# Later low parts of weights, latent key rotation on GpSimd, and attention tiles of layer B in one row

## The chip, the cores and the metric

The kernel runs on one core of a Trainium2 chip. The metric is the time of one execution on the device, in microseconds (us); several runs are taken and their median counts. Besides, the hardware profiler records one execution; all rows below are from that record. TensorE (PE) does the matrix products, VectorE (DVE) and ScalarE (ACT) the work on rows of 128 partitions, GpSimd (POOL) some arithmetic, SyncE (SP) issues the transfers.

## What is computed

512 tokens of width 1024 go through two blocks: layer A (mLSTM and a memory attention), layer B (latent attention and a memory attention), then a second block with differential attention, cross attention and an MLP. The change lies for the most part in layer B. Cut to that layer:

```python
def shared_kv(x, positions, kv_norm, w_kv_a, kv_lat_norm, w_kv_b, k_gain):
    h = rmsnorm(x, kv_norm)
    c_kv, k_pe = split_cols(h @ w_kv_a, [KV_LORA, QK_ROPE])            # 256, 64
    kv = (rmsnorm(c_kv, kv_lat_norm) @ w_kv_b).reshape(bsz, s, B_HEADS, QK_NOPE + V_HEAD)
    k_nope, v = kv[..., :QK_NOPE], kv[..., QK_NOPE:]
    k = jnp.concatenate([k_nope, broadcast(k_pe)], axis=-1)
    k = rmsnorm(k, k_gain)
    return concatenate([k[..., :QK_NOPE], rope(k[..., QK_NOPE:], positions)]), v

def mla_layer(x, positions, k_sh, v_sh, ...):
    h = rmsnorm(x, norm_g)
    q_lat, z, mq, mz = split_cols(h @ w_in, [Q_LORA, B_WIDTH, MEM_WIDTH, MEM_WIDTH])
    q = (rmsnorm(q_lat, q_lat_g) @ w_q_up).reshape(bsz, s, B_HEADS, QK_HEAD)   # 8 heads
    q = rmsnorm(q, q_gain);  q = concatenate([q[..., :QK_NOPE], rope(q[..., QK_NOPE:], positions)])
    attn = chunk_causal_attention(q, k_sh, v_sh)     # tiles of 128 queries, keys up to the tile's end
    y_b = attn * silu(z)
    y_mem = memory_attention(mq, mz, mk, mv, mq_gain)                            # 4 heads, 256 keys
    return x + concatenate([y_b, y_mem]) @ w_out
```

## The kernel before, in words

Every product with a weight is computed at nearly float32 accuracy from two fp32r parts. A weight chunk (two blocks of 128 rows, up to 512 columns) is fetched into one of two raw buffers, ScalarE writes its high part (step `split`, line 1549, in two halves), and VectorE the low part, raw minus high (line 1938, `sb_w_split<-sb_raw,sb_w_split`, in two halves, each waiting for ScalarE's half). TensorE then does three matmuls per block of rows and output tile: high by high, high by low, low by high (lines 1246 to 1248 or 1251 to 1253). There are three buffers for split chunks, so the split of chunk n+2 stands at the start of chunk n; the fetch into a raw buffer waits for the low part that was made from it.

One list of steps, made by `order_of_work` with the class `Plan`, sets the order on all five engines: each engine walks through the list and does its share of each step, in order. `Plan.product` puts the rows of a product, and after some of them calls `Plan.step`, which may put a step from one of two side lanes. A side step goes in when what it needs stands in the list already and a distance (`lag`, in a planner's nanoseconds of TensorE work) from the last one is reached. If a product needs the result of side steps that aren't in the list yet, `need` forces them in, one after the other, with no rows between.

The side work of layer B:

- `rounds` lays out an attention tile by tile. A tile's scores (`msc` of the memory attention, `asc` of the latent attention) are computed on TensorE into one of PSUM banks 4 to 7, VectorE takes the row maximum (line 2153) and scales it (1941), ScalarE takes the exponential (step `exp`, line 1695), VectorE divides by the sum (`norm`, lines 2159 and 1941), TensorE turns the result over (`mtp`, `atp`, line 1209) and ScalarE copies it out. A round holds the turning of tile n-2, `norm` of tile n-1 and the scores of tile n; `exp` of tile n stands a distance later. When a head's four tiles are turned, its values product (`mval` at line 1345, `aval` at 1425) follows, then VectorE's product with the gate and the two parts of y (`ysplit`). `mem_b` and `mla` call `rounds` once for each pair of heads, so each pair ends with three rounds without new scores.
- Each pair of latent heads has a preparation in seven steps, `prep0` to `prep6`, in the other lane: sums of squares on ScalarE (line 1517, four squares each in prep0 to prep3), transposes of q and k on TensorE, normalisation on VectorE, and rotation of q's last 64 columns on GpSimd (prep4 and prep5, line 2441). prep6 turns the rotated q over; ScalarE copies it out in two halves. The scores of the pair's first tile wait for all of these copies.
- `kpe` rotates the 64 shared key columns for all four token tiles, on VectorE.

Products in the order of the list: qlB, ckvB, mk1, mqB, mv1, mzB0, mzB1, kvB0, quB0, zB0, kvB1, quB1, zB1, kvB2, quB2, zB2, kvB3, quB3, zB3, outB0, outB1. outB takes y's 12 blocks of 128 in the order 0 to 3, 8 to 11, 4 to 7; blocks 0 to 7 are the heads' values.

## Time and profile before

| what | us |
|---|---|
| median of 3 runs (lowest, highest) | 1583.37 (1582.98, 1588.41) |
| the profiled execution | 1586.22 |
| its span from first to last instruction | 1584.4 |
| TensorE busy in the span | 1535.1 (97%) |
| VectorE, ScalarE, GpSimd busy | 887.2, 707.6, 223.0 |

An engine's idle time costs only where the engine that sets the end waits for it. TensorE is the one that is nearly always busy, so a row of TensorE with a bracket, the idle time ahead of it and what ended it, is the thing to look for. Transposes and single matmuls are pipelined, so the gap between starts is some 0.17 us more than the idle time in the bracket.

### The profile page before, as it was taken

How to read it: one execution, taken by the hardware profiler on the slowest of the kernel's cores; microseconds unless marked ns; L12 is line 12 of the kernel's file. 1: busy time of each engine (PE TensorE's matmuls, PEld its weight loads, DVE VectorE, ACT ScalarE, POOL GpSimd, SP SyncE). 2: the span in 40 equal slices, each digit the busy share in tenths (PEclk: the TensorE clock that was granted, in tenths of full speed). 3: DMA queues.
4: the chain of work that ended last, by engine and by line, in shares of the span. 5: the costliest groups of instructions: out<-in, count | busy, mean ns of one | idle time of the engine just before them, and what ended most of it. 6: DMA issues, size and time to landing. Idle time of an engine off the chain costs nothing.

```text
span 1584.4 us, 19220 instructions
## 1 busy us (share of the span) xinstructions
PE 1535.1 (97%) x7128; PEld 1245.0 (79%) x7128; DVE 887.2 (56%) x1747; ACT 707.6 (45%) x1611; POOL 223.0 (14%) x192
## 2 busy tenths in 40 slices
PE   7999999999999999999899999999999999999997
PEld 5887778887898777777588877788778888888886
DVE  6467485657465566666457567664446433444343
ACT  6554343334355767665334444443344423333241
POOL 3202020202120003222022005120002000000001
PEclk9999999999999999999999999999999999999998
DMA  6522122323424221112133221233232333333331
GB/s 193 160 67 80 53 81 67 94 67 120 119 74 142 81 61 55 52 57 67 41 120 100 87 67 54 67 116 111 93 93 68 107 100 100 93 94 106 94 94 66
DMA packets 89069, 141.04 MB, mean 89 GB/s; under 512 B 6417, under 2 KB 36497, under 8 KB 88977
## 3 DMA queue, kind: packets, MB, share of 16 engines
q1 hardware_dynamic: 88256, 139.02, 28.8%
q8 instruction: 56, 0.92, 0.2%
q10 hardware_dynamic: 720, 0.81, 0.2%
q14 instruction: 37, 0.30, 0.1%
HBM read 137.71 MB, written 2.10 MB: 88 GB/s over the span
## 4 chain that ended last, share of the span: by engine, by line
PE 78%; DVE 9%; ACT 5%; issue 3%; POOL 3%; DMA 2%; SPq 0%; POOLq 0%; ACTq 0%; DVEq 0%
PE banks L1246 16%; PE banks L1248 16%; PE banks L1247 16%; PE banks L1251 6%; PE banks L1253 6%; PE banks L1252 6%; DVE sb_w_split L1938 2%; PE banks L1209 2%; DVE sb_arena L1947 2%; ACT sb_junk L1517 2%; PE banks L1372 1%; ACT sb_w_split L1549 1%; PE banks L1425 1%; PE banks L1488 1%; DVE sb_arena L1941 1%
## 5 line engine op out<-in xcount | busy, mean ns | idle before, releaser
L1938 DVE TENSOR_TENSOR sb_w_split<-sb_raw,sb_w_split 128x512 fp32r<-128x512 f32 (+4 forms) x530 | 344.4, 692 | 365.5 <-ACT sb_w_split L1549 364.8
L1549 ACT ACTIVATE sb_w_split<-sb_raw 128x512 fp32r<-128x512 f32 (+4 forms) x530 | 288.1, 592 | 424.3 <-PE banks L1248 307.7
L1246 PE MATMUL banks<-sb_actA,sb_w_split 128*128 128x512 f32 x672 | 276.4, 411 | 2.4 <-DVE sb_arena L1938 2.1
L1248 PE MATMUL banks<-sb_actA,sb_w_split 128*128 128x512 f32 x672 | 263.1, 392 | 0.0
L1247 PE MATMUL banks<-sb_actA,sb_w_split 128*128 128x512 f32 x672 | 262.1, 390 | 0.0
L1246 PE MATMUL banks<-sb_actB,sb_w_split 128*128 128x512 f32 (+1 forms) x640 | 248.5, 388 | 1.5 <-DVE sb_actB L1938 1.5
L1248 PE MATMUL banks<-sb_actB,sb_w_split 128*128 128x512 f32 (+1 forms) x640 | 242.9, 380 | 0.0
L1247 PE MATMUL banks<-sb_actB,sb_w_split 128*128 128x512 f32 (+1 forms) x640 | 242.6, 379 | 0.0
L1251 PE MATMUL banks<-sb_w_split,sb_actA 128*128 128x512 f32 (+1 forms) x384 | 153.7, 400 | 13.3 <-DVE sb_w_split L1938 9.9
L2458 POOL TENSOR_TENSOR sb_arena<-sb_arena 128x512 f32<-128x512 f32 x43 | 63.4, 1474 | 686.5 <-ACT sb_arena L1590 684.1
L1246 PEld LDWEIGHTS banks<-sb_actA,sb_w_split 128*128 128x128 f32 x672 | 126.5, 188 | 32.3 <-issue 7.2
L1252 PE MATMUL banks<-sb_w_split,sb_actA 128*128 128x512 f32 (+1 forms) x384 | 149.3, 389 | 0.0
L1253 PE MATMUL banks<-sb_w_split,sb_actA 128*128 128x512 f32 (+1 forms) x384 | 149.3, 389 | 0.0
L1248 PEld LDWEIGHTS banks<-sb_actA,sb_w_split 128*128 128x128 f32 x672 | 126.2, 188 | 27.3
L1247 PEld LDWEIGHTS banks<-sb_actA,sb_w_split 128*128 128x128 f32 x672 | 126.7, 189 | 24.5 <-issue 1.0
L1246 PEld LDWEIGHTS banks<-sb_actB,sb_w_split 128*128 128x128 f32 x640 | 120.6, 188 | 26.1 <-issue 2.5
L1247 PEld LDWEIGHTS banks<-sb_actB,sb_w_split 128*128 128x128 f32 x640 | 120.7, 189 | 22.8 <-issue 1.4
L1248 PEld LDWEIGHTS banks<-sb_actB,sb_w_split 128*128 128x128 f32 x640 | 120.5, 188 | 22.8
L2449 POOL TENSOR_TENSOR sb_small<-sb_small,sb_cons 128x4 f32<-128x4 f32 (+3 forms) x30 | 42.1, 1404 | 548.9 <-DVE sb_small L1944 548.9
L1251 PEld LDWEIGHTS banks<-sb_w_split,sb_actA 128*128 128x128 f32 x384 | 72.9, 190 | 27.6 <-issue 13.7
L1253 PEld LDWEIGHTS banks<-sb_w_split,sb_actA 128*128 128x128 f32 x384 | 73.0, 190 | 14.4
L1251 PE MATMUL banks<-sb_w_split,sb_actB 128*128 128x512 f32 (+2 forms) x208 | 81.9, 394 | 2.4 <-DVE sb_w_split L1938 1.6
(217 smaller groups left out, 2084.7 us busy)
## 6 DMA issues: line engine op xcount, KB each, us to landing
sb_raw<-in_a_w_in SPq DMA_DIRECT2D x66, 256.0 KB, 3.0
sb_raw<-in_w_up SPq DMA_DIRECT2D x32, 512.0 KB, 3.7
sb_raw<-in_w_down SPq DMA_DIRECT2D x32, 512.0 KB, 3.8
sb_raw<-in_w_in SPq DMA_DIRECT2D x24, 512.0 KB, 3.6
sb_raw<-in_mem_w_kv SPq DMA_DIRECT2D x16, 512.0 KB, 3.8
sb_raw<-in_w_ckv SPq DMA_DIRECT2D x16, 512.0 KB, 3.7
sb_raw<-in_a_w_in SPq DMA_DIRECT2D x15, 512.0 KB, 3.8
sb_raw<-in_a_w_out SPq DMA_DIRECT2D x12, 512.0 KB, 3.8
```

The source lines that it names most:

```text
L1209: t = pe.op.transpose(v.ps[0:rows, place.bank, n * P:(n + 1) * P], block, v.ident)
L1246: pe.op.matmul(out, hi[:, cs], x.hi(k), start=i == 0, stop=False)
L1247: pe.op.matmul(out, hi[:, cs], x.lo(k), start=False, stop=False)
L1248: t = pe.op.matmul(out, lo[:, cs], x.hi(k), start=False, stop=last_i)
L1251: pe.op.matmul(out, x.hi(k)[:, cs], hi, start=i == 0, stop=False)
L1252: pe.op.matmul(out, x.hi(k)[:, cs], lo, start=False, stop=False)
L1253: t = pe.op.matmul(out, x.lo(k)[:, cs], hi, start=False, stop=last_i)
L1517: t = act.op.activation(v.junk[:, 0:src.shape[-1]], src, ACT.Square, accum_out=out)
L1549: act.op.activation(hi[:, cs], raw[:, cs], ACT.Copy).then_inc(act.mark(m("w_hi"), 2 * n + part + 1), 1)
L1938: dve.op.tensor_tensor(out, a, b, op).then_inc(dve.mark(*mark) if mark else dve.tick(), 1)
L2449: pool.op.tensor_tensor(v.stat(root, n), v.stat(mean, n), v.con("minus_half", 0, n), ALU.pow).then_inc(m.at("rstd", step)[0], 1)
L2458: pool.op.tensor_tensor(total, total, v.square_of(norm, n)[1], ALU.add).then_inc(pool.mark(signal, value), 1)
```

## The change

Four edits of the list, and one step on another engine.

1. A new step `low` does VectorE's low part; `split` keeps ScalarE's high part. `low` of a chunk goes into the list at the next call of `Plan.step`, ahead of the next side step, or at the latest ahead of the next `split`. For products with 256 tokens it stays at once behind `split`.
2. `kpe` runs on GpSimd: one product with the gain over all four tiles in place of four, then the same six operations of the rotation.
3. `mla` and `mem_b` call `rounds` once over all heads. What a tile needs (its pair's prep6) is asked for tile by tile.
4. Lags of the preparation: prep0 2600 in place of 4000, prep6 5000 in place of 6500, the others 1600 in place of 2600.

```diff
+    def low(self):
+
+        if self.held_low is not None:
+            self.put(("low", self.held_low))
+            self.held_low = None
+
     def step(self):
+        self.low()
         if self.soon:
...
+                self.low()
                 self.put(("split", self.n_split))
+                self.held_low = self.n_split
+                if pr.tokens < SEQ:
+                    self.low()
...
-            needed = list(after) if n == 0 else []
+            needed = list(after(*units[n])) if n < len(units) else []
...
-    def mla(h0):
-        rounds(0, [(h, j) for h in (h0, h0 + 1) for j in range(TT)], "asc", "atp",
-               lambda u: [("aval", *u), ("ysplit", "yB", *u)], [("prep6", h0 // 2)],
+    def mla():
+        rounds(0, [(h, j) for h in range(B_HEADS) for j in range(TT)], "asc", "atp",
+               lambda u: [("aval", *u), ("ysplit", "yB", *u)], lambda h, j: [("prep6", h // 2)],
...
-    def mem_b(h0):
-        rounds(0, [("B", h, i) for h in (h0, h0 + 1) for i in range(TT)], "msc", "mtp", lambda u: [("mval", *u)],
-               [("hnscale", "mqB"), ("hnt", "mk1", 3)], [("silu", f"mzB{h0 // 2}", 1)], lag=1300, wait=1000)
+    def mem_b():
+        rounds(0, [("B", h, i) for h in range(MEM_HEADS) for i in range(TT)], "msc", "mtp", lambda u: [("mval", *u)],
+               lambda layer, h, i: [("hnscale", "mqB"), ("hnt", "mk1", 3)],
+               lambda u: [("silu", f"mzB{u[1] // 2}", 1)], lag=1300, wait=1000)
...
-            p.side(1, after, (f"prep{n}", q), lag={0: 4000, 6: 6500}.get(n, 2600))
+            p.side(1, after, (f"prep{n}", q), lag={0: 2600, 6: 5000}.get(n, 1600))
...
     (vector_program)
-        if kind == "split":
+        if kind == "low":
...
-        elif kind == "kpe":
-            g = v.prob[:, 0, 0:TT * QK_ROPE].rearrange("p (i n) -> p i n", i=TT)
-            gain = v.rows[:, ROW["k_gain_pe"]:ROW["k_gain_pe"] + QK_ROPE]
-            for i in range(TT):
-                dve.wait_ge(*m.evicted("ckvB", i))
-                tensor(g[:, i, :], v.ckv[:, i, KV_LORA:320], gain, ALU.mult)
-            dve.settle()
-            dve.wait_ge(*m.at("cos", ("rotab2",)))
-            rope(g, v.kpe, v.prob[:, 1, 0:TT * HALF].rearrange("p (i n) -> p i n", i=TT), v.cosB, v.sinB,
-                 *m.at("kpe", step))
     (gpsimd_program)
+        elif kind == "kpe":
+            g = v.prob[:, 0, 0:TT * QK_ROPE].rearrange("p (i n) -> p i n", i=TT)
+            tmp = v.prob[:, 1, 0:TT * HALF].rearrange("p (i n) -> p i n", i=TT)
+            gain = v.rows[:, ROW["k_gain_pe"]:ROW["k_gain_pe"] + QK_ROPE]
+            pool.wait_ge(m("dma_params"), 48)
+            for i in range(TT):
+                pool.wait_ge(*m.evicted("ckvB", i))
+            pool.settle()
+            tensor(g, v.ckv[:, :, KV_LORA:320], gain.unsqueeze(1).broadcast_to([P, TT, QK_ROPE]), ALU.mult)
+            pool.settle()
+            pool.wait_ge(*m.at("cos", ("rotab2",)))
+            s1, s2, o1, o2 = g[:, :, 0:HALF], g[:, :, HALF:], v.kpe[:, :, 0:HALF], v.kpe[:, :, HALF:]
+            tensor(o1, s1, v.cosB, ALU.mult)
+            tensor(tmp, s2, v.sinB, ALU.mult)
...
+            tensor(o2, o2, tmp, ALU.add, *m.at("kpe", step))
```

What that makes of the order, at three places. The first is TensorE at the end of outB0, the last tiles of head 7 (`atp` is line 1209, `asc` 1408, 1410 and 1225, `aval` 1425, rows of outB0 1246 to 1248). Before:

```order
L1209 MATMUL banks<-sb_cons,sb_arena 128x128
L1408 MATMUL banks<-sb_arena 128x384
L1410 MATMUL banks<-sb_arena 128x384
L1225 MATMUL banks<-sb_masks 128x128
L1209 MATMUL banks<-sb_cons,sb_arena 128x128 x2
L1408 MATMUL banks<-sb_arena 128x512
L1410 MATMUL banks<-sb_arena 128x512
L1225 MATMUL banks<-sb_masks 128x128
L1209 MATMUL banks<-sb_cons,sb_arena 128x128 x7
L1425 MATMUL banks<-sb_arena 128x512
...
L1246 MATMUL banks<-sb_actB,sb_w_split 128x512
```

Now, from the second tile's `atp` on (the same code is at lines 1222, 1421, 1423, 1238, 1438 and 1259 to 1261):

```order
L1222 MATMUL banks<-sb_cons,sb_arena 128x128 x2
L1421 MATMUL banks<-sb_arena 128x512
L1423 MATMUL banks<-sb_arena 128x512
L1238 MATMUL banks<-sb_masks 128x128
L1259 MATMUL banks<-sb_actB,sb_w_split 128x512
...
L1222 MATMUL banks<-sb_cons,sb_arena 128x128 x3
L1259 MATMUL banks<-sb_actB,sb_w_split 128x512
...
L1222 MATMUL banks<-sb_cons,sb_arena 128x128 x4
L1259 MATMUL banks<-sb_actB,sb_w_split 128x512
...
L1438 MATMUL banks<-sb_arena 128x512
```

Between the steps of the last tiles there were no rows of the product; now there are four rows (of three matmuls each) after the last scores, two after `atp` of three blocks and two after that of four. `aval` of head 7 stood directly behind `atp`, with the chunk's first row after it; now the last row of the chunk before and then that first row follow it.

The second place is VectorE while TensorE is at mzB1 and kvB0, in the memory attention's first tiles (`norm` is 2159 and the 1941 with 128x256, the maximum 2153, low parts `sb_w_split`). Before:

```order
L2153 TENSOR_REDUCE sb_small<-banks 128x1
L1941 TENSOR_SCALAR sb_small<-sb_small 128x1
L1938 TENSOR_TENSOR sb_w_split<-sb_raw,sb_w_split 128x384 x2
L2159 RECIPROCAL sb_small<-sb_small 128x1
L1941 TENSOR_SCALAR sb_actB_plain<-sb_actB_plain,sb_small 128x256
L2153 TENSOR_REDUCE sb_small<-banks 128x1
L1941 TENSOR_SCALAR sb_small<-sb_small 128x1
L1938 TENSOR_TENSOR sb_arena<-sb_arena,sb_rows 128x64 x4
...
L1938 TENSOR_TENSOR sb_arena<-banks,sb_arena 128x512 x2
L1947 SCALAR_TENSOR_TENSOR sb_arena<-sb_cons,sb_arena 128x512
L2159 RECIPROCAL sb_small<-sb_small 128x1
```

Now, at the same tiles:

```order
L2166 TENSOR_REDUCE sb_small<-banks 128x1
L1954 TENSOR_SCALAR sb_small<-sb_small 128x1
L2172 RECIPROCAL sb_small<-sb_small 128x1
L1954 TENSOR_SCALAR sb_actB_plain<-sb_actB_plain,sb_small 128x256
L2166 TENSOR_REDUCE sb_small<-banks 128x1
L1954 TENSOR_SCALAR sb_small<-sb_small 128x1
L1951 TENSOR_TENSOR sb_w_split<-sb_raw,sb_w_split 128x384 x2
L1951 TENSOR_TENSOR sb_arena<-banks,sb_arena 128x512 x2
L1960 SCALAR_TENSOR_TENSOR sb_arena<-sb_cons,sb_arena 128x512
L2172 RECIPROCAL sb_small<-sb_small 128x1
```

The low part moved behind the next `norm` and maximum, into the place where the ten operations of `kpe` stood.

The third place is TensorE at the start of outB0, where the last pair's prep6 (four transposes) stands. Before:

```order
L1225 MATMUL banks<-sb_masks 128x128
L1246 MATMUL banks<-sb_actB,sb_w_split 128x512
L1247 MATMUL banks<-sb_actB,sb_w_split 128x512
L1248 MATMUL banks<-sb_actB,sb_w_split 128x512
L1209 MATMUL banks<-sb_cons,sb_arena 128x128 x4
L1246 MATMUL banks<-sb_actB,sb_w_split 128x512
...
L1209 MATMUL banks<-sb_cons,sb_arena 128x128 x2
L1408 MATMUL banks<-sb_arena 128x512
```

Now:

```order
L1259 MATMUL banks<-sb_actB,sb_w_split 128x512
L1260 MATMUL banks<-sb_actB,sb_w_split 128x512
L1261 MATMUL banks<-sb_actB,sb_w_split 128x512
L1222 MATMUL banks<-sb_cons,sb_arena 128x128 x7
L1421 MATMUL banks<-sb_arena 128x128
L1423 MATMUL banks<-sb_arena 128x128
L1238 MATMUL banks<-sb_masks 128x128
```

prep6 stood in outB0 behind the scores of tile 2 of head 5, and the scores of head 6, which wait for its copies, came 12 rows later. Now prep6 follows outB0's first four rows, and behind its four transposes come three of an `atp` and at once head 6's first scores.

## Rows read from the trace of the kernel before

**Rows 1.** The page, busy time per engine: busy us (share of the span) xinstructions.

```profile
PE 1535.1 (97%) x7128; PEld 1245.0 (79%) x7128; DVE 887.2 (56%) x1747; ACT 707.6 (45%) x1611; POOL 223.0 (14%) x192
```

**Rows 2.** Waits of TensorE, 545 to 790 us: line, releaser, total, times, longest.

```profile
PE banks L1209 <- DVE sb_arena L1941: 6.3, 6, 2.2
PE banks L1209 <- DVE sb_actB_plain L1941: 6.0, 6, 1.7
```

**Rows 3.** Timeline, end of outB0: start, duration, instruction, xcount, [idle before it].

```profile
768.06 2.32 PE L1425 MATMUL banks<-sb_arena 128*128 128x512 f32 x8
...
773.28 0.44 PE L1209 MATMUL banks<-sb_cons,sb_arena 128*128 128x128 f32 x2 [1.44 <-DVE sb_arena L1941]
...
778.21 0.66 PE L1209 MATMUL banks<-sb_cons,sb_arena 128*128 128x128 f32 x4 [2.15 <-DVE sb_arena L1941]
779.64 4.09 PE L1425 MATMUL banks<-sb_arena 128*128 128x512 f32 x8 [0.78 <-ACT sb_arena L1816]
...
783.76 0.69 DVE L1947 SCALAR_TENSOR_TENSOR sb_arena<-banks,sb_arena 128x512 f32<-128x512 f32 x1 [5.62 <-PE banks L1425]
...
785.90 0.50 PE L1246 MATMUL banks<-sb_actB,sb_w_split 128*128 128x512 f32 x1 [1.47 <-DVE sb_actB L1938]
```

**Rows 4.** The chain that ended last, in order of time: one matmul of outB0.

```profile
764.97 0.23 PE banks L1247
```

**Rows 5.** Stretch at that place: us, busy per engine, granted clock (PEclk).

```profile
780.00:785.00 5.00, 4.43 (x11) 2.22 (x9) 0.69 (x1) 0.51 (x1) 0.00 (x0) 0.68 0.01 3
```

**Rows 6.** Timeline, mzB1 and kvB0: VectorE, then TensorE.

```profile
557.35 1.03 DVE L1938 TENSOR_TENSOR sb_w_split<-sb_raw,sb_w_split 128x384 fp32r<-128x384 f32 x2 [1.20 <-ACT sb_w_split L1549]
...
559.33 0.62 DVE L1938 TENSOR_TENSOR sb_arena<-sb_arena,sb_rows 128x64 f32<-128x64 f32 x4
559.99 1.68 DVE L1938 TENSOR_TENSOR sb_arena<-sb_arena 128x128 f32<-128x128 f32 x6
...
551.32 0.44 PE L1209 MATMUL banks<-sb_cons,sb_actB_plain 128*128 128x128 f32 x2 [0.76 <-DVE sb_actB_plain L1941]
...
555.62 0.44 PE L1209 MATMUL banks<-sb_cons,sb_actB_plain 128*128 128x128 f32 x2 [1.35 <-DVE sb_actB_plain L1941]
...
564.17 0.44 PE L1209 MATMUL banks<-sb_cons,sb_actB_plain 128*128 128x128 f32 x2 [1.67 <-DVE sb_actB_plain L1941]
```

**Rows 7.** GpSimd, whole span, groups by line and form: products of two tensors.

```profile
L2480 POOL TENSOR_TENSOR sb_arena<-sb_arena 128x496 f32<-128x496 f32 x4 | 5.0, 1249 | 0.3
...
L2477 POOL TENSOR_TENSOR sb_arena<-sb_arena 128x16 f32<-128x16 f32 x4 | 0.9, 222 | 0.3
```

**Rows 8.** Timeline, zB2: VectorE and GpSimd at the same time.

```profile
675.93 2.33 DVE L1938 TENSOR_TENSOR sb_w_split<-sb_raw,sb_w_split 128x384 fp32r<-128x384 f32 x2
...
676.91 5.63 POOL L2441 TENSOR_TENSOR sb_arena<-sb_arena 128x256 f32<-128x256 f32 x6
```

**Rows 9.** Timeline of TensorE, zB0 and zB2: the longest idle of each.

```profile
599.81 0.44 PE L1209 MATMUL banks<-sb_cons,sb_actB_plain 128*128 128x128 f32 x2 [1.72 <-DVE sb_actB_plain L1941]
...
672.38 0.44 PE L1209 MATMUL banks<-sb_cons,sb_arena 128*128 128x128 f32 x2 [1.07 <-DVE sb_arena L1941]
```

**Rows 10.** Groups by line and form, ScalarE, zB2 (656 to 679 us).

```profile
L1517 ACT ACTIVATE sb_junk<-sb_arena 128x192 f32<-128x192 f32 x8 | 2.9, 363 | 0.5
L1807 ACT ACTIVATE sb_arena<-banks,sb_cols 128x512 f32<-128x512 f32 x4 | 2.7, 670 | 0.0
```

**Rows 11.** Timeline of GpSimd, last pair: from the sums of q on.

```profile
716.68 2.01 POOL L2449 TENSOR_TENSOR sb_small<-sb_small,sb_cons 128x8 f32<-128x8 f32 x1 [5.62 <-DVE sb_small L1944]
...
720.02 6.24 POOL L2441 TENSOR_TENSOR sb_arena<-sb_arena 128x256 f32<-128x256 f32 x6
```

**Rows 12.** Stretch of zB2: busy per engine (PE PEld DVE ACT POOL), clock, DMA.

```profile
656.00:679.00 23.00, 21.84 (x107) 16.19 (x106) 13.89 (x32) 16.76 (x58) 6.92 (x6) 1.00 0.19 61
```

**Rows 13.** Timeline, end of ozA0 in layer A: VectorE, then TensorE.

```profile
134.08 4.29 DVE L1938 TENSOR_TENSOR sb_w_split<-sb_raw,sb_w_split 128x512 fp32r<-128x512 f32 x4
...
141.41 0.69 PE L1251 MATMUL banks<-sb_w_split,sb_actA 128*128 128x512 f32 x1 [2.98 <-DVE sb_arena L1947]
```

More of the change, by code:

```diff
@@ L378, in advance @@
                 self.take(lane)
+    def low(self):
+        if self.held_low is not None:
+            self.put(("low", self.held_low))
+            self.held_low = None
     def step(self):
+        self.low()
         if self.soon:
@@ L478, in finish @@
         total = len(self.chunks)
-        self.order = [s for s in self.order if s[0] not in ("split", "fetch") or s[1] < total]
+        self.order = [s for s in self.order if s[0] not in ("split", "low", "fetch") or s[1] < total]
         self.chunk_of = {c: n for n, c in enumerate(self.chunks)}
@@ L545, in order_of_work @@
     p.put(("split", 0))
+    p.put(("low", 0))
     p.put(("fetch", 2))
@@ L549, in order_of_work @@
     p.put(("split", 1))
+    p.put(("low", 1))
     p.n_split, p.n_fetch = 2, 3
@@ L584, in order_of_work @@
     rounds(0, units, "msc", "mtp", lambda u: [("mval", *u)],
-           [("hnscale", "mqA"), ("silu", "mzA", 3), ("hnt", "mk0", 3)], lag=6000)
+           lambda layer, h, i: [("hnscale", "mqA"), ("silu", "mzA", 3), ("hnt", "mk0", 3)], lag=6000)
     def mlstm_head(h):
@@ L662, in latents @@
             after = [("asc", 2 * q - 3, TT - 1)] if q >= 2 and n == 0 else [("ysplit", "yB", 3)] if (q, n) == (3, 4) else ()
-            p.side(1, after, (f"prep{n}", q), lag={0: 4000, 6: 6500}.get(n, 2600))
+            p.side(1, after, (f"prep{n}", q), lag={0: 2600, 6: 5000}.get(n, 1600))
     def gated(name):
         p.product(name, (), lambda j: [(("silu", name, j),)])
-    mem_b(0)
-    mem_b(2)
+    mem_b()
     p.need(("nrow", "b"))
@@ L675, in order_of_work @@
     gated("zB0")
-    for n in range(4):
-        mla(2 * n)
+    mla()
     latents(1)
@@ L758, in order_of_work @@
         for n in (2 * g, 2 * g + 1):
-            rounds(n % 2, [(n, i) for i in range(TT)], "csc", "ctp", lambda u: [("cval", *u)], (),
+            rounds(n % 2, [(n, i) for i in range(TT)], "csc", "ctp", lambda u: [("cval", *u)], lambda h, i: (),
                    [("ev", f"cvD{g}", MT - 1)])
@@ L2482, in gpsimd_program @@
             pool.op.tensor_tensor(u[:, 0:16], edge, u[:, 0:16], ALU.subtract).then_inc(pool.mark(*m.at("pooled", step)), 1)
+        elif kind == "kpe":
[12 more added lines that the diff above has]
+            tensor(tmp, s2, v.sinB, ALU.mult)
+            pool.settle()
+            tensor(o1, o1, tmp, ALU.subtract)
+            tensor(o2, s2, v.cosB, ALU.mult)
+            pool.settle()
+            tensor(tmp, s1, v.sinB, ALU.mult)
+            pool.settle()
+            tensor(o2, o2, tmp, ALU.add, *m.at("kpe", step))
         elif kind in ("prep4", "prep5"):
```

## The prediction

> **What bounds the kernel now.** I began with the page: TensorE is busy in 1535.1 of 1584.4 us, no other engine in more than 56% of the span [rows 1]. The change removes no work of TensorE, so all that it can give or take is TensorE's idle time, some 49 us in all, and the question is which waits lie where the order changes. The waits of TensorE in layer B come next [rows 2]: two kinds make up 12.3 us, the turning of a latent tile (`atp`) that waits for VectorE's `norm`, and the same for the memory attention (`mtp`), six times each. The timeline then shows where these stand. The end of outB0 is the worst place [rows 3]: idle times of 1.44, 2.15, 0.78 and 1.47 us follow one another, because head 7's last steps are forced in with no rows of the product between them. In a single matmul's price, 0.23 us [rows 4], a row of the product is 0.69 us, so there is room to fill. The idle time costs more than itself: the granted clock over the next 5 us is 0.68 on average [rows 5], so the engine spent part of that stretch at the lower of its two levels (1.2 and 2.4 GHz) after having stood idle, and head 7's values product took 4.09 us where head 6's took 2.32 [rows 3]. The other places are the start of the memory attention [rows 6], the z products [rows 9], and the end of ozA0 in layer A [rows 13].
>
> **The tail of outB0.** Before: idle 1.44 + 2.15 + 0.78 + 1.47 = 5.8, a short wait of 0.2 more, and 4.09 - 2.32 = 1.8 in the slow values product; 7.8 together. Now four rows (2.8 us) stand behind the last scores. From the start of the scores in question to the `atp` that needs them TensorE now takes 773.28 to 778.21, that is 4.9 us, of which 2.15 were waited; 2.8 us of rows cover that wait. The tile before gets rows as well, and the two rows (1.4 us) between the last `atp` and the values product cover the 0.78 for ScalarE's copy. What is left is the wait for y's last block: from the end of the values product (779.64 + 4.09 = 783.73) to 785.90 is 2.17 us, of which two rows now fill 1.38. That leaves 0.8 idle, and 0.17 more between starts, so 0.95. With the long idle times gone I take the clock to stay up. Gain 7.8 - 0.95 = 6.9; from 6.0, if the clock still falls for half of that product, to 7.6.
>
> **The start of the memory attention, mzB1 and kvB0.** Four `mtp` wait here; three of them are in [rows 6], with 0.76, 1.35 and 1.67, and a shorter one stands between; with the 0.17 between starts, 4.8 us. The low part (1.03) and `kpe` (0.62 + 1.68) stand ahead of the `norm` in question. For the last two of the four, moving the low part behind the next maximum and taking 2.3 us of `kpe` off VectorE is more than the wait, so both go: -2.3. The first two stay: they wait for the exponential's own chain, not for a low part of their own. Against it stands `kpe` on GpSimd, which the trace doesn't show. The nearest rows are products of 496 columns at 1.25 and of 16 at 0.22 us [rows 7], which by a straight line puts one of 256 at 0.75 and the six of 128 at 0.45 each: 3.5 us (1.5 if all cost 0.22, 8.8 if all cost 1.25). It starts after the gate's sums, where VectorE has low parts with two operands in SBUF to do. Such a low part takes 2.33 us in two halves while GpSimd rotates [rows 8], and 1.03 while it is idle [rows 6]: 0.65 for each half. One to two halves fall into `kpe`'s time: +0.65 to +1.3 at the first tile, I take 1.1. Gain 1.2; from a loss of 0.5, if the last two are late for another reason (the exponential), to 3, if nothing collides.
>
> The Trainium skill ("SBUF — State Buffer", Who interferes with whom) says that a VectorE instruction with two SBUF inputs and a GpSimd instruction that reads SBUF exclude one another, the later one being stopped for the whole of the other. The 2.33 against 1.03 agrees in kind. It speaks against this part of the change: by the full stop, two halves and two products of the gate would lose up to 1.25 each in `kpe`'s time, the start's gain would be gone, and the sum below would be 5.3 instead of 6.5; the forecast's range holds that.
>
> **The z products.** In zB0, one `mtp` waits 1.72 us [rows 9] and another 0.2; with the pairs in one row, the scores of head 3's first tile now follow without a break, and need the bank that ScalarE's exponential of the tile four back empties, behind a denser preparation: I put that wait at 1.9 against 2.3 now. Gain 0.4; from -1.9 (both waits stand) to 1.9. In zB1, waits below 0.4 us go in part: gain 0.4 (0 to 1).
>
> In zB2, before: an `atp` waits 1.07 [rows 9], with short ones 1.5 in all. Now prep1's sums of squares stand ahead of a tile's exponential, and the scores of the next pair's first tile stand directly behind prep6's four transposes. ScalarE has to copy these out first: two copies at 0.67 [rows 10], a third operation of that size ahead of them, and 0.2 for the hand-over, so 2.2. The tile behind prep1's four squares (0.36 each, 1.45 together [rows 10]) is late by half of that, 0.75; with a short one of 0.35 the stage has 3.3. Loss 1.8; from a gain of 1 to a loss of 3.5.
>
> In zB3 and the start of outB0, GpSimd is the chain: from the sums of q at 716.68 to the rotated q at 726.26 (720.02 + 6.24) it takes 9.6 us [rows 11], and 1.9 us go by on TensorE, ScalarE and VectorE ahead of that: 11.5 us from prep3. The order wants prep6 some 9.3 us of TensorE's work behind prep3 (its rows and side steps at their prices). The distances of prep4 to prep6 add up to 8.2 us now and to 11.7 before. So TensorE waits about 2.0 at prep6, and then about 1.1 for the copies, as in zB2 with something between; it has 1.6 now, of which one `atp` with 1.06. Loss 1.5; from a gain of 1.2, if GpSimd is as quick as in the first pair, to a loss of 3.5.
>
> Denser preparation also puts more low parts beside GpSimd's rotation: two halves more at 0.65 [rows 8, 6], of which 1.0 reaches TensorE (0 to 1.5).
>
> **Layer A and the rest.** At the end of ozA0, VectorE does four halves of low parts in 4.29 us, and the eviction that TensorE waits for comes after; 2.98 idle [rows 13]. The low part of one chunk moves behind that eviction: 2.1 us less ahead of it, of which the exponential's own chain gives back a little. Gain 2.0 with a short wait of 0.4 nearby (0 to 3.4). Elsewhere the low part has no step of VectorE between it and its old place. Its new place delays the fetch into the raw buffer by less than one side step, and SP's queue holds nothing else that TensorE waits for there; TensorE wants the low part two chunks later. I cost this at nothing; what hides it is that distance. If it were gone, a row would wait for a low part, some 1.0 us each.
>
> **The sum.** -6.9 (tail) - 1.2 (start) - 0.4 (zB0) - 0.4 (zB1) + 1.8 (zB2) + 1.5 (zB3) + 1.0 (beside GpSimd) - 2.0 (layer A) = -6.6. Against the profiled execution, 1586.22, that is 1579.6. It stood 2.85 above the median of the runs, so I forecast a median of 1577.0, which is 0.4% faster.
>
> **Rivals.**
> First, the shorter distances cost nothing: prep6 arrives in time, and the three losses of zB2, zB3 and GpSimd (4.3) don't appear, while the waits that both stages have now (1.5 and 1.6) go. Then -6.6 - 4.3 - 3.1 = -14.0, or 1569.4. For it speaks that TensorE idles only 1.2 us of the 23 in zB2 now [rows 12] with ScalarE at 16.8; against it, that GpSimd's 9.6 us [rows 11] are longer than the new distance.
>
> Second, only the tail counts: the low part's and `kpe`'s moves turn into waits for the next thing on the same chain. Then the tail's -6.9 and the losses of +4.3 stand alone: -2.6, or 1581. For it speaks that the first `mtp` waits are there with no low part ahead of them; against it, the order on VectorE, where `norm` now stands ahead.
>
> Third, slower: ScalarE becomes the bound in the z stages. It is busy in 16.8 of 23 us of zB2 [rows 12]. There are 16 groups of four squares (four pairs, prep0 to prep3), 1.45 us each [rows 10]. If each now falls directly ahead of a tile's exponential, so that the two rounds between scores and turning no longer hide it, TensorE waits 16 x 1.45 = 23.2 us, less the two waits near 1.07 that it has now, less the tail's 6.9: +14, or 1597.6. It decides from the point where a round's work on TensorE is shorter than a group, an exponential and `norm` together; a round with its rows is some 3 us, so most groups fit.
>
> Fourth, the change doesn't do what it says, because the new order leaves the tail's forced steps; the order on TensorE shows rows there, so I give it no chance of its own.
>
> **How the numbers follow.** The forecast's case (1574 to 1580) gets 0.50, the first rival (1567 to 1574) 0.22, the second (1580 to 1583) 0.22, the third 0.06. About 0.5% is what a measurement of this kernel can tell from no change: 1575.45 and 1591.3 are the bounds. Faster is the first rival and a third of the forecast's case, 0.38; slower the third, 0.06; the same the rest, 0.56. The range leaves out the lower half of the first rival, the upper end of the second and the third: 1571 to 1582.
>
> **What would show it.** In the profile after, no idle time over 1 us should stand in the last 15 us of outB0, head 7's values product should take about 2.3 us, and a wait near 0.8 should stand for y's last block. At mzB1 and kvB0 two `mtp` waits should be gone, and low parts longer than 1.03 should lie beside GpSimd's `kpe` of some 3.5 us. At the last pair's prep6 a wait for GpSimd of about 2 us should stand, and one for ScalarE's copies at the scores behind it; without these the first rival is right. Waits for ScalarE at most of the tiles in the z stages would show the third. The prediction is wrong if a new wait of several us stands where the order didn't change, or if the clock falls at a place where it didn't before.

## The result, and the profile after

The changed kernel takes 1592.41 us (median of 9 runs, 1588.94 to 1594.43), the kernel before 1586.53 (9 runs, 1582.98 to 1589.63): a ratio of 1.0042, 95% interval 1.0032 to 1.0052. By that ratio it is slower by 6.7 us; 1577.0 was forecast, and the range ended at 1582. The profiled execution's span grew from 1584.4 to 1591.3 us, by 6.9.

The page, against [rows 1]:

```profile
PE 1540.6 (97%) x7128; PEld 1246.4 (78%) x7128; DVE 887.1 (56%) x1737; ACT 708.2 (45%) x1611; POOL 227.1 (14%) x199
```

Waits of TensorE from 545 to 800 us of the changed kernel (line, releaser, total, times, longest), against [rows 2]:

```profile
PE banks L1222 <- DVE sb_actB_plain L1954: 3.7, 3, 1.9
PE banks L1222 <- DVE sb_arena L1954: 2.5, 3, 1.4
PE banks L1344 <- ACT sb_actB_plain L1708: 1.8, 1, 1.8
PE banks L1421 <- ACT sb_actB_plain L1818: 1.5, 1, 1.5
PE banks L1222 <- POOL sb_arena L2444: 1.5, 1, 1.5
PE banks L1421 <- ACT sb_arena L1818: 1.4, 1, 1.4
PE banks L1259 <- DVE sb_arena L1951: 1.2, 1, 1.2
PE banks L1222 <- DVE sb_arena L1951: 0.8, 1, 0.8
```

The two kinds of [rows 2], 6.3 and 6.0, are down to 2.5 and 3.7. New kinds stand beside them: scores (L1344, L1421) that wait for ScalarE, prep6 (L1222) for GpSimd, rows for an eviction.

The tail of outB0, timeline of TensorE, against [rows 3]:

```profile
784.75 0.49 PE L1222 MATMUL banks<-sb_cons,sb_arena 128*128 128x128 f32 x3
...
788.30 2.32 PE L1438 MATMUL banks<-sb_arena 128*128 128x512 f32 x8
...
792.79 0.51 PE L1259 MATMUL banks<-sb_actB,sb_w_split 128*128 128x512 f32 x1 [0.78 <-DVE sb_actB L1951]
```

This part came out as forecast. No `atp` waits, the last values product takes 2.32 in place of 4.09, and 0.78 us are left ahead of y's last block.

To see where more than these 7 us went, I took each matmul's distance to the next one, less the median distance for its kind, and summed this over the list's stages. The sums explain the spans: 57.6 and 64.4 us, a difference of 6.8. Kinds can be told apart in more than one way, which moves a difference of the table by up to 0.4. In us:

| stage | before | changed | difference | forecast |
|---|---|---|---|---|
| layer A | 9.4 | 12.9 | +3.5 | -2.0 |
| qlB to mv1 | 2.8 | 3.4 | +0.6 | 0 |
| mzB0 to quB0 | 5.3 | 4.0 | -1.3 | -1.2 |
| zB0 to quB1 | 2.7 | 5.2 | +2.5 | -0.4 |
| zB1 to quB2 | 2.0 | 2.7 | +0.7 | -0.4 |
| zB2 to quB3 | 2.5 | 5.7 | +3.2 | +1.8, and +1.0 beside GpSimd |
| zB3 and outB0's first 28 rows | 3.4 | 9.3 | +5.9 | +1.5 |
| outB0's last 20 rows | 9.2 | 1.3 | -7.9 | -6.9 |
| from outB1 on | 20.4 | 20.0 | -0.4 | 0 |

From mzB0 on, the stages of layer B repeat within some 0.2 us between executions with the same order there (but for the clock, last section). The first two lines and the last don't. Up to qlB's first matmul, TensorE takes 439.7 us in the kernel before, 438.0 to 441.6 in the nine below that order layer A as it does, 442.0 in e1 and 442.9 in the changed kernel. From outB1's first matmul to the last one it takes 784.0 to 789.1 over all kernels, whose order there differs at most in low parts. So a single profile says much on layer B and little on the rest.

### The profile page after: what moved, and what is told of

It is laid out like the page before. It is cut to its first block, busy times and chain, and to the rows that moved or that the text cites. A ratio compares the mean times of both kernels' runs of the same rounds, so it can differ in the third digit from the quotient of the medians.

```text
span 1591.3 us, 19222 instructions
## 1 busy us (share of the span) xinstructions
PE 1540.6 (97%) x7128; PEld 1246.4 (78%) x7128; DVE 887.1 (56%) x1737; ACT 708.2 (45%) x1611; POOL 227.1 (14%) x199
## 4 chain that ended last, share of the span: by engine, by line
PE 74%; DVE 11%; ACT 6%; issue 4%; POOL 3%; DMA 2%; SPq 0%; POOLq 0%; ACTq 0%; DVEq 0%
PE banks L1259 16%; PE banks L1261 16%; PE banks L1260 16%; PE banks L1264 5%; PE banks L1266 5%; PE banks L1265 5%; DVE sb_w_split L1951 4%; DVE sb_arena L1960 3%; ACT sb_junk L1530 3%; PE banks L1222 2%; PE banks L1385 1%; ACT sb_w_split L1562 1%; DVE sb_arena L1954 1%; PE banks L1501 1%; PE banks L1421 1%
## 5 line engine op out<-in xcount | busy, mean ns | idle before, releaser
L1951 DVE TENSOR_TENSOR sb_w_split<-sb_raw,sb_w_split 128x512 fp32r<-128x512 f32 (+4 forms) x530 | 353.5, 708 | 220.5 <-ACT sb_w_split L1562 220.0
L1264 PEld LDWEIGHTS banks<-sb_w_split,sb_actA 128*128 128x128 f32 x384 | 73.5, 191 | 28.2 <-issue 12.2
L1951 DVE TENSOR_TENSOR sb_x_res<-sb_x_res,banks 128x512 f32<-128x512 f32 x64 | 43.9, 686 | 91.7 <-PE banks L1261 91.7
```

What stands on the lines that cost most here:

```text
L1264: pe.op.matmul(out, x.hi(k)[:, cs], hi, start=i == 0, stop=False)
L1951: dve.op.tensor_tensor(out, a, b, op).then_inc(dve.mark(*mark) if mark else dve.tick(), 1)
```

## The experiments

All ratios are to the kernel before, from runs on the same chip; the medians of before were 1586.04 (e1 to e4), 1586.24 (e5 to e7), 1586.11 (e8 to e10) and 1584.03 (e11, e12). A ratio compares all runs and need not be that of the medians; two ratios that differ by less than some 0.0017 (2.7 us) are not told apart by these runs. My theory was that each new wait hangs on one edit at its place; the rivals stand in the expectations.

### The edits one by one: e1 to e4

**e1**, the low parts alone (`low` and its calls, VectorE's branch):

```diff
     def step(self):
+        self.low()
         if self.soon:
...
+                self.low()
                 self.put(("split", self.n_split))
+                self.held_low = self.n_split
...
-        if kind == "split":
+        if kind == "low":
```

> The kernel before with only the low parts later. Theory 1 (a later low part falls into chains that TensorE waits for): the waits of the changed kernel in layer A come back here, 2.5 us at head 1's first scores and 0.8 us in vA2, and layer A is 3 to 4 us longer than before; the whole is 2 to 4 us slower, 1588 to 1591 beside 1586.5. Rival (those waits come from one execution to the next, not from the order): layer A as before within 1 us, and the whole within 1 us of before.

Measured: 1590.23, ratio 1.0031 (1.0019 to 1.0043). Theory 1 holds. The waits in layer A are back, 2.54 and 0.71 us, and so is one behind ozA0 that I hadn't listed, 2.09 (0.80 in the changed kernel); layer A's sum is 11.9 against 9.4, zB0's 4.3 against 2.7.

**e2**, one row each, with old distances:

```diff
-            needed = list(after) if n == 0 else []
+            needed = list(after(*units[n])) if n < len(units) else []
...
-    for n in range(4):
-        mla(2 * n)
+    mla()
```

> The kernel before with only the attentions of layer B in one row each. Theory 1 (the row pays at the end of outB0, and the losses of the z stages come from the low parts and the shorter distances): the tail's waits go, -7 us, and new waits at the first scores of a pair take 0 to 3 us back, so 3 to 7 us faster, 1579.5 to 1583.5. Rival (the row itself costs in the z stages, since the three rounds without new scores were the slack in which a pair's preparation was done): the tail's 7 us are given back at the pairs' first scores, and the whole is within 1.5 us of before.

Measured: 1590.73, ratio 1.0040 (1.0025 to 1.0055), slower than either expected. The z stages go from 7.2 to 13.2, zB3 with outB0's first 28 rows from 3.4 to 6.9, and the tail keeps 4.0, since with old distances the last tiles still come late; timeline of TensorE there:

```profile
785.53 2.39 PE L1424 MATMUL banks<-sb_arena 128*128 128x512 f32 x8 [1.71 <-ACT sb_arena L1815]
...
790.10 0.50 PE L1245 MATMUL banks<-sb_actB,sb_w_split 128*128 128x512 f32 x1 [1.47 <-DVE sb_actB L1937]
```

So the row itself costs in the z stages, as the rival says, and theory 1's clean tail belongs to row and distances together.

**e3**, the distances alone:

```diff
-            p.side(1, after, (f"prep{n}", q), lag={0: 4000, 6: 6500}.get(n, 2600))
+            p.side(1, after, (f"prep{n}", q), lag={0: 2600, 6: 5000}.get(n, 1600))
```

> The kernel before with only the preparation at shorter distances. Theory 1 (the denser preparation puts ScalarE's squares and copies ahead of tiles): waits at tiles behind the sums of squares of 0.8 us and more appear in zB0, zB1 and zB2, and the whole is 2 to 5 us slower, the tail's 7 us unchanged. Rival (the waits of the z stages come from the row, which leaves no round without new scores): within 1 us of before.

Measured: 1604.90, ratio 1.0121 (1.0107 to 1.0134): 19 us, far more than expected. The z stages go from 7.2 to 23.0. Timelines of VectorE and TensorE in zB2 of e3:

```profile
681.81 0.17 DVE L1944 TENSOR_SCALAR sb_small<-sb_small 128x8 f32<-128x8 f32 x1 [2.86 <-ACT sb_junk L1517]
682.90 1.29 DVE L1938 TENSOR_TENSOR sb_w_split<-sb_raw,sb_w_split 128x512 fp32r<-128x512 f32 x2 [0.33 <-ACT sb_w_split L1549]
684.31 1.16 DVE L1941 TENSOR_SCALAR sb_arena<-sb_arena,sb_small 128x256 f32<-128x256 f32 x1
...
685.52 0.44 PE L1209 MATMUL banks<-sb_cons,sb_arena 128*128 128x128 f32 x2 [1.67 <-DVE sb_arena L1941]
687.10 2.07 PE L1408 MATMUL banks<-sb_arena 128*128 128x512 f32 x2 [1.13 <-ACT sb_arena L1695]
```

VectorE waits 2.86 us for the sums of squares (`sb_junk` is ScalarE's), and behind that wait stand, in its order, a low part and only then the tile's `norm` (684.31); `atp` waits 1.67 us for it, and the next scores for an exponential. This is my third rival's mechanism, ScalarE's squares in front of tiles, reached by way of VectorE. In one row the tiles stand elsewhere between the preparation's steps and it costs less (e5). Shorter distances are not needed for it: in zB2 of e2, with the old ones, VectorE waits 2.86 us for the squares as well, and an `atp` 2.15 behind it:

```profile
683.24 0.18 DVE L1943 TENSOR_SCALAR sb_small<-sb_small 128x8 f32<-128x8 f32 x1 [2.86 <-ACT sb_junk L1516]
...
688.08 0.44 PE L1208 MATMUL banks<-sb_cons,sb_arena 128*128 128x128 f32 x2 [2.15 <-DVE sb_arena L1940]
```

**e4**, the key rotation alone, with the bodies that the diff of the change shows:

```diff
     (vector_program)
-        elif kind == "kpe":
...
     (gpsimd_program)
+        elif kind == "kpe":
```

> The kernel before with only the key rotation on GpSimd. Theory 1 (it takes 2.3 us off VectorE and slows VectorE's work beside it): the fourth wait of the memory attention's start, 1.67 us, goes, the first, 0.76 us, becomes about 1.9; the whole within 1 us of before. Rival (beside GpSimd nothing is slower that TensorE waits for): the first wait stays at 0.8, and the whole is 1.5 to 2.5 us faster.

Measured: 1585.17, ratio 1.0000 (0.9989 to 1.0010). Theory 1 holds to the number; the first `mtp` waits 1.79 in place of the 0.76 of [rows 6], the fourth doesn't wait:

```profile
553.25 0.44 PE L1209 MATMUL banks<-sb_cons,sb_actB_plain 128*128 128x128 f32 x2 [1.79 <-DVE sb_actB_plain L1941]
...
557.56 0.44 PE L1209 MATMUL banks<-sb_cons,sb_actB_plain 128*128 128x128 f32 x2 [1.35 <-DVE sb_actB_plain L1941]
```

### What of it the low parts cost: e5 and e6

**e5** is the changed kernel with each low part beside its high part; **e6** has them at once in layer A only. The edits of the changed kernel, first e5's, then e6's:

```diff
     def step(self):
-        self.low()
         if self.soon:
...
-        if kind == "low":
+        if kind == "split":
```

```diff
-                if pr.tokens < SEQ:
+                if pr.tokens < SEQ or ("enter", "outA1") not in self.done:
                     self.low()
```

> The changed kernel with each low part back beside its high part, the other three edits kept. Theory 1 (the later low parts cost about 3 us in layer A and 1 to 2 in zB0): layer A as in the kernel before, and the whole 3 to 6 us under the changed kernel's 1592.4, so 1586 to 1589, the tail of outB0 still without waits over 1 us. Rival (the low parts' place matters for layer A alone and helps in layer B, where norm stands ahead of them): the start of the memory attention and the z stages get worse by 2 us or more, and the whole is 1590 to 1593.

> The changed kernel with the low parts at once in layer A, later from layer B on. Theory 1 (layer A's new waits come from low parts that moved behind the first eviction of a head, beside GpSimd's products): the wait of 2.5 us at head 1's first scores is back at 1.3 and the one of 0.8 us in vA2 is gone; layer A is 3 us shorter than in the changed kernel, layer B as there, and the whole 1589 to 1590.5. Rival (layer A's waits don't hang on that): layer A and the whole as in the changed kernel, 1591.5 to 1593.5.

Measured: e5 1588.61, ratio 1.0018 (1.0005 to 1.0032); e6 1587.90, ratio 1.0006 (0.9993 to 1.0018). Theory 1 holds for layer A: of the 6.7 us 5.7 go in e6, where the low parts are at once there (3 to 8 by the two intervals). Layer B is not decided. The rival of e5 names the right places, since the start of the memory attention has 4.4 without the later low parts (e5) and 4.0 with them (e6), zB0 5.8 and 5.1, zB2 6.6 and 5.7; but zB3 with outB0's first 28 rows has 6.3 without and 7.9 with them, the clock's fall there included, and the ratios of e5 and e6 are not told apart.

The place in layer A, head 1's first scores; VectorE, GpSimd and TensorE of the changed kernel:

```profile
216.04 2.18 DVE L1951 TENSOR_TENSOR sb_w_split<-sb_raw,sb_w_split 128x512 fp32r<-128x512 f32 x2
...
232.72 3.08 DVE L1951 TENSOR_TENSOR sb_w_split<-sb_raw,sb_w_split 128x512 fp32r<-128x512 f32 x2
...
233.83 1.42 POOL L2573 TENSOR_TENSOR sb_arena<-sb_arena 128x512 f32<-128x512 f32 x1
...
235.40 2.04 PE L1373 MATMUL banks<-sb_arena 128*128 128x512 f32 x2 [2.52 <-POOL sb_arena L2573]
```

and of e6, in which TensorE reaches this place 1.6 us later:

```profile
216.19 1.29 DVE L1951 TENSOR_TENSOR sb_w_split<-sb_raw,sb_w_split 128x512 fp32r<-128x512 f32 x2
...
231.38 1.29 DVE L1951 TENSOR_TENSOR sb_w_split<-sb_raw,sb_w_split 128x512 fp32r<-128x512 f32 x2 [1.30 <-ACT sb_w_split L1562]
...
234.49 1.15 POOL L2573 TENSOR_TENSOR sb_arena<-sb_arena 128x512 f32<-128x512 f32 x1
...
235.79 1.10 PE L1373 MATMUL banks<-sb_arena 128*128 128x512 f32 x2 [1.34 <-POOL sb_arena L2573]
```

In e6 no low part takes over 1.29 here. In the changed kernel one stands at 216.04 beside GpSimd's products of the convolution and takes 2.18, so all that VectorE does behind it is 0.9 us later, down to the step that lets GpSimd begin its last two products; the next, moved behind an eviction, meets the last of these: it takes 3.08, and the product 1.42 in place of 1.15. Together that is the 1.2 us by which the scores wait longer, 2.52 against 1.34. The place repeats well: 2.52 and 2.54 in the two kernels with later low parts here, 1.34 to 1.36 in the twelve others. After the wait the scores run at half the pace (2.04 for two against 1.10; the granted clock is 0.50 from 235.4 to 238.8 us), which e1, with a wait of 2.54, does not show: that part is the clock (last section). In vA2 a low part of 2.18 stands straight ahead of the eviction that TensorE waits for (0.77 us there, 0.71 in e1, nothing in the others).

### The tail without the rest: e7

```diff
-            by_bank = kk > 1 and (last or c == 0 and first)
+            by_bank = kk > 1 and (last and name != "outB0" or c == 0 and first)
...
+            ("atp", 7, 0): 36, ("exp", "asc", 7, 2): 37, ("atp", 7, 1): 38, ("exp", "asc", 7, 3): 39, ("atp", 7, 2): 40,
+            ("atp", 7, 3): 41, ("aval", 7): 42}
...
     p.product("outB0", first=False)
+    spread()
```

`spread` takes the side steps from head 6's first scores on, in their order, and puts each group behind the row of outB0 whose number the table gives.

> The kernel before in which only outB0's last rows are spread between the steps of heads 6 and 7, three or two rows to a tile in place of four and none, and block 6 ahead of block 7; nothing else is moved. Theory 1 (the tail's waits are paid for with rows at hand): of the 7.8 us there some 3 stay, and the whole is 3.5 to 5.5 us faster, 1581 to 1583. Rival (VectorE and ScalarE set the pace of the tiles, and with fewer rows each tile waits): the waits move to the tiles of head 6, and the whole is within 1.5 us of before.

Measured: 1583.34, ratio 0.9977 (0.9966 to 0.9988): faster by 2.9 us in the medians and 3.6 by the ratio, at the lower end of the 3.5 to 5.5 expected. Theory 1 holds: the profile's tail is 4.9 in place of 9.2, and the tiles of head 6 don't wait. Timeline of TensorE there:

```profile
777.18 0.66 PE L1237 MATMUL banks<-sb_cons,sb_arena 128*128 128x128 f32 x4 [1.97 <-DVE sb_arena L1969]
...
783.18 0.50 PE L1274 MATMUL banks<-sb_actB,sb_w_split 128*128 128x512 f32 x1 [1.47 <-DVE sb_actB L1966]
```

The old order of the z stages with rows in the tail beats the whole change.

### The first scores of a pair: e8 and e9

**e8** is e6 with e7's `by_bank` line and a distance between prep6 and a new pair's first scores; **e9** puts the last prep6 later as well:

```diff
-            p.side(lane, needed, *group, lag=lag)
+            pair = scores == "asc" and n and n < len(units) and n % (2 * TT) == 0
+            if pair:
+                p.side(lane, needed, lag=0)
+                needed = []
+            p.side(lane, needed, *group, lag=2000 if pair else lag)
...
-            p.side(1, after, (f"prep{n}", q), lag={0: 2600, 6: 5000}.get(n, 1600))
+            p.side(1, after, (f"prep{n}", q), lag={0: 2600, 6: 5000 + (1500 if q == 3 else 0)}.get(n, 1600))
```

> The kernel of e6 (low parts at once in layer A) in which the first scores of a new pair of heads come at least 2 us of TensorE's work after prep6, and the last block of outB0 follows block 6 whole, so that the tail keeps its rows. Theory 1 (in one row the first scores stand directly behind prep6 and wait for ScalarE's copies): the waits of 1.5 us at head 4's and 1.4 us at head 6's first scores go, GpSimd's wait of 1.5 us at prep6 stays, and the whole is 2 to 3.5 us under e6's 1587.9, 1584.4 to 1586. Rival (ScalarE has too much to do at that place, whatever follows): waits of the same sum appear at the tiles around, and the whole is 1587 to 1589.

> As e8, with the last pair's prep6 1.5 us later. Theory 1 (TensorE stands at prep6 until GpSimd's rotation is done): GpSimd's wait of 1.5 us goes as well; since the last tiles come later, up to 1 us of it comes back in the tail; 1583.5 to 1586. Rival (the rotation itself is late because VectorE's low parts and GpSimd slow each other, and moves on): GpSimd's wait stays over 1 us, and the whole is as e8 or slower.

Measured: e8 1584.66, ratio 0.9991 (0.9982 to 1.0001); e9 1585.57, ratio 0.9999 (0.9989 to 1.0010). For e8 theory 1 holds at most in the sum, by the ratios 2.4 us under e6, which is within the noise, and not in the places. In zB2, head 4's wait is gone, but a tile of head 3 now waits for its exponential. In outB0, head 6's is down from 1.40 to 0.99 only, and prep6's wait for GpSimd, which I expected to stay, is gone; TensorE in zB2 and outB0, then GpSimd:

```profile
677.13 0.70 PE L1425 MATMUL banks<-sb_arena 128*128 128x256 f32 x2 [1.78 <-ACT sb_arena L1712]
...
739.23 0.46 PE L1425 MATMUL banks<-sb_arena 128*128 128x128 f32 x2 [0.99 <-ACT sb_arena L1822]
...
723.70 2.01 POOL L2456 TENSOR_TENSOR sb_small<-sb_small,sb_cons 128x8 f32<-128x8 f32 x1 [5.39 <-DVE sb_small L1961]
```

Moving the tiles of heads 3 and 4 moved the last pair's preparation in the list too: GpSimd begins its part at 723.70, in e6 at 728.92. e9 leaves no wait at head 6 (outB0's head 3.6), and the tail takes it back (5.5): what the preparation gets, the last tiles lose.

### A version that beats both: e10 to e12

**e10** is e7 with `kpe` on GpSimd and low parts later in four products; **e11** is the kernel before with only heads 4 to 7 in one row (the arguments of `mla` are the first head and their count), e8's distance, and the tail spread from head 5's last tiles on; **e12** is e11 with e10's edits:

```diff
-    for n in range(4):
-        mla(2 * n)
+    mla(0, 2)
+    mla(2, 2)
+    mla(4, 4)
...
+                self.held_low = self.n_split
+                if name not in ("qkA0", "mzB1", "kvB0", "gC0"):
+                    self.low()
```

> The kernel of e7 (old order and distances, spread tail) with the key rotation on GpSimd and later low parts in four products alone: qkA0, mzB1, kvB0 and gC0. Theory 1 (each edit pays where no chain that TensorE waits for follows the low part): the last two waits of the memory attention's start go (-1.3 together with the first's growth), the one of 1.9 us at gC0's end shrinks to 0.8, the one of 0.6 us ahead of ozA0 goes; 2 to 3 us under e7's 1583.3, so 1580.3 to 1581.5. Rival (these are below what differs from one execution to the next): 1582.5 to 1584.

> The kernel before (old distances, low parts at once, key rotation on VectorE) with heads 4 to 7 alone in one row, head 6's first scores 2 us of work behind prep6, and outB0's rows spread between the tiles of heads 6 and 7. Theory 1 (in the row the losses come where scores stand directly behind prep6 and where the preparation is dense, the gain from the rows in the tail): the z stages wait as before, no wait over 0.5 us at head 6's first scores, and of the tail's waits 1 to 1.5 us stay; 2 to 4 us under e7, 1579.5 to 1581.5. Rival (the tiles at three rows each wait for VectorE and ScalarE): waits of 1 us and more at the tiles of heads 6 and 7, and the whole as e7, 1583, or slower.

> e11 with the key rotation on GpSimd and later low parts in qkA0, mzB1, kvB0 and gC0, as in e10. Theory 1 (these places pay): 2 to 2.5 us under e11, by 1.3 in the memory attention's start, 0.7 ahead of ozA0 and 0.9 in gC0. Rival (as e10 against e7 showed 0.3 us in the medians, the gains are taken back elsewhere): within 1 us of e11.

Measured: e10 1582.99, ratio 0.9972 (0.9963 to 0.9981); e11 1578.63, ratio 0.9964 (0.9952 to 0.9977); e12 1575.97, ratio 0.9950 (0.9937 to 0.9964), 8 us faster than before and, by the ratios, 0.9% faster than the changed kernel. e11's z stages wait as in the kernel before (2.7, 2.0, 2.5), outB0's first 28 rows 3.5, its tail 1.8. In e12 one wait over 0.3 us is left in outB0; timeline of TensorE:

```profile
777.60 0.50 PE L1294 MATMUL banks<-sb_actB,sb_w_split 128*128 128x512 f32 x1 [0.79 <-DVE sb_actB L1986]
```

On the small edits the runs say little: from e11 to e12 it is 2.7 us by the medians (2.2 by the ratios, as expected), from e7 to e10 0.3 (0.8), and in both cases the intervals overlap. The profiles show that one of the three places gives nothing: the wait ahead of ozA0 (0.40) goes, but the next one, at vA0's first row, grows from 2.97 to 3.64 in e10 and from 2.95 to 3.63 in e12. The other two places are shorter in both.

## Why the prediction failed, step by step

**The tail** was right: 6.9 forecast, 7.9 by the sums, with the 0.95 that was to stay (0.78 idle). One reason given was incomplete. The rows came there from one row and shorter distances together; with one row alone the tail keeps 4.0 (e2). And the 1.8 us for the slow values product hang on the execution that was profiled: e3 has the same four waits in its tail (1.45, 2.16, 0.78, 1.47), a granted clock of 1.00 behind them, and a values product of 2.39.

**The memory attention's start** was right: -1.2 forecast, -1.3 measured, with the last two waits gone and the first longer by 1.1. GpSimd's rotation took 0.88 + 3.71 us where 3.5 was estimated. VectorE beside it is slower by the 1.1 that was taken, but in part by luck: about half of it is a step that the prediction didn't list, two small `TENSOR_SCALAR` that take 0.79 us beside GpSimd's first product and 0.25 in the kernel before. GpSimd, VectorE and TensorE:

```profile
549.48 0.88 POOL L2444 TENSOR_TENSOR sb_arena<-sb_arena,sb_rows 128x256 f32<-128x256 f32 x1
550.43 3.71 POOL L2444 TENSOR_TENSOR sb_arena<-sb_arena 128x128 f32<-128x128 f32 x6
...
549.68 0.79 DVE L1954 TENSOR_SCALAR sb_small<-sb_small 128x16 f32<-128x16 f32 x2
...
556.21 0.44 PE L1222 MATMUL banks<-sb_cons,sb_actB_plain 128*128 128x128 f32 x2 [1.88 <-DVE sb_actB_plain L1954]
```

The rule of the Trainium skill that was weighed there ("SBUF — State Buffer", Who interferes with whom) would have left no gain; the trace shows the collision and, since it met only the first tile, a gain all the same. (By the prediction's own sum of 6.6 the figure without that gain is 5.4, not 5.3.)

**Layer A** was the step with the largest miss: +3.5 against -2.0. Two sentences failed. The first is that at the end of ozA0 the moved chunk leaves "2.1 us less ahead of it", of the eviction, worth a gain of 2.0. The 4.29 us of [rows 13] are not two equal parts: the chunk that stayed takes 3.08 beside GpSimd's products, so only 1.2 went, and 2.43 us are left of the wait of 2.98. And the chunk that moved stands behind the first eviction but ahead of the second, for which TensorE waits next. VectorE and TensorE of the changed kernel:

```profile
140.04 3.08 DVE L1951 TENSOR_TENSOR sb_w_split<-sb_raw,sb_w_split 128x512 fp32r<-128x512 f32 x2
...
139.81 0.76 PE L1264 MATMUL banks<-sb_w_split,sb_actA 128*128 128x512 f32 x1 [2.43 <-DVE sb_arena L1960]
...
143.51 0.50 PE L1264 MATMUL banks<-sb_w_split,sb_actA 128*128 128x512 f32 x1 [0.80 <-DVE sb_arena L1960]
```

From the end of ozA0 to the second of these rows of TensorE it is 6.1 us here and in e1 (there at full clock, with a second wait of 2.09), and 4.4 to 5.7 in the ten kernels that order this place as before (5.4 and more where the clock fell there as it did here, 4.5 and less where it didn't). So the gain of 2.0 was a loss, of some 0.5 us here and 1.7 in e1.

The second is that elsewhere "the low part has no step of VectorE between it and its old place". I had compared the places of layer B and one place of layer A. In head 1's last chunk the low part moved behind the first eviction, and the steps queued behind it were the ones that TensorE waits for; e1 and e6 show it.

**zB0, zB1 and zB2**: +2.5, +0.7, +3.2 against -0.4, -0.4, +2.8. The loss in zB2 came near its size. The wait for a bank in zB0 was sized well, 1.9 with a measured 1.78; ScalarE, VectorE and TensorE there:

```profile
592.28 0.21 DVE L1954 TENSOR_SCALAR sb_small<-sb_small 128x1 f32<-128x1 f32 x1
...
594.72 0.67 ACT L1820 ACTIVATE sb_arena<-banks,sb_cols 128x512 f32<-128x512 f32 x1
595.29 0.55 ACT L1708 ACTIVATE sb_actB_plain<-banks,sb_small 128x256 f32<-128x256 f32 x1
...
595.99 0.70 PE L1344 MATMUL banks<-sb_actB_plain 128*128 128x256 f32 x2 [1.78 <-ACT sb_actB_plain L1708]
```

The maximum was ready at 592.49, and the exponential starts at 595.29, behind four squares and a copy. What I left out is that the old waits don't all go where a new one comes, and that prep3 waits too (0.82, VectorE's normalisation behind a `norm` and a low part). It is the third rival's mechanism, which I gave 0.06, in part of the tiles. The sum had the shorter distances as its source and priced the row only at a pair's first scores; but the row alone adds 6.0 us in these three stages (e2), the distances alone 15.8 (e3), both with the rest of the change 6.4.

**zB3 and outB0's start**: +5.9 against +1.5. TensorE, VectorE and GpSimd of the changed kernel:

```profile
739.19 0.50 PE L1259 MATMUL banks<-sb_actB,sb_w_split 128*128 128x512 f32 x1 [1.20 <-DVE sb_arena L1951]
...
742.31 0.98 PE L1222 MATMUL banks<-sb_cons,sb_arena 128*128 128x128 f32 x7 [1.47 <-POOL sb_arena L2444]
744.69 0.77 PE L1421 MATMUL banks<-sb_arena 128*128 128x128 f32 x2 [1.40 <-ACT sb_arena L1818]
...
733.84 4.69 DVE L1951 TENSOR_TENSOR sb_w_split<-sb_raw,sb_w_split 128x512 fp32r<-128x512 f32 x4 [1.09 <-ACT sb_w_split L1562]
...
735.77 6.49 POOL L2444 TENSOR_TENSOR sb_arena<-sb_arena 128x256 f32<-128x256 f32 x6
```

The two waits that I named came at their size: 1.47 for GpSimd (2.0 forecast) and 1.40 for the copies (1.1). Two things were missing. Four halves of low parts take 4.69 us beside GpSimd's rotation, and the evictions of zB3 behind them come late for outB0's third row (1.20; 1.17 in e5, so the later place is not the reason). The sum's 1.0 for low parts beside GpSimd had two halves and no eviction behind them. And the clock fell after these waits (last section): e5, with the same three waits and no fall, has 6.3 in this stage in place of 9.3.

**The level** was a mistake of its own. I took the median of three runs, 1583.37, as the kernel's time and the profiled execution as 2.85 us above it. With 9 runs the median is 1586.53, where the profiled execution (1586.22) stood; 3.2 of the 15.4 us between forecast and measurement are this.

## What to carry to other kernels

When a step is moved by a rule ("at the next call of `step`") and not by hand, list every place where another step of the same engine came to stand ahead of it, and ask of each who waits for that; three such places in layer A took back some 3.5 us by the sums, about half of what the tail had gained. Where work is packed closer to fill one hole, take the rows for it from where nothing waits: spreading rows over the last tiles alone took 4.3 of the tail's 9.2 us away (e7), and 7.4 with heads 4 to 7 in one row (e11), with nothing lost ahead of it, while all heads in one row (e2) and a closer preparation (e3) each cost more in the z stages than the tail gave. And take the level of a kernel from more than three runs when the effect is half a per cent.

## What the runs showed of the hardware

The same waits cost differently from one execution to the next, by the clock that followed. Stretches of the changed kernel at outB0's start, then of e5, whose three long waits there differ by less than 0.05 us (PE busy is the second number, the granted clock the third from the end):

```profile
740.00:745.00 5.00, 2.13 (x12) 1.46 (x11) 5.00 (x7) 4.95 (x10) 2.78 (x3) 0.90 0.25 95
745.00:750.00 5.00, 5.00 (x16) 3.96 (x16) 2.39 (x10) 0.61 (x3) 0.00 (x0) 0.50 0.32 105
```

```profile
740.00:745.00 5.00, 2.76 (x17) 2.34 (x18) 4.96 (x11) 3.54 (x7) 1.32 (x2) 1.00 0.07 11
745.00:750.00 5.00, 5.00 (x26) 4.10 (x25) 2.13 (x8) 2.84 (x7) 0.00 (x0) 1.00 0.28 103
```

After some 4 us of idle time in 10, TensorE ran the next stretch at the lower of its two levels in one execution (0.50, 1.2 GHz) and at full clock in the other; in e6, with the same three waits once more, the stretch from 740 to 745 us has 0.66. So a sum of idle times is a lower bound of what waits cost, and a single profile can't give the rest. The runs give an estimate: the span times what its mean granted clock lacks to 1 is 12.2 us on average over the 9 runs of the changed kernel, and 9.1 to 10.7 in the four groups of runs of the kernel before, beside which the experiments ran. By that some 2 of the 6.7 us came with the clock.

VectorE's subtract of two SBUF operands, 128x512, took 0.65 us with GpSimd idle (1.29 for two) and 1.58 beside one of GpSimd's products. Of the pair of 2.18 in layer A the first stands alone and the second beside GpSimd, as this row of VectorE shows; of the pairs of 3.08 both do.

```profile
216.64 1.58 DVE L1951 TENSOR_TENSOR sb_w_split<-sb_raw,sb_w_split 128x512 fp32r<-128x512 f32 x1
```

I had priced this from [rows 8], at 0.65 for each half, and for layer B alone; it weighed most in layer A.
